# Two of four block differences moved from VectorE to GpSimd in a two-layer transformer trunk

## The reference

```
def _swiglu(h, w_gate_up, w_down):
    gu = h @ w_gate_up
    g, u = jnp.split(gu, 2, axis=-1)
    return (jax.nn.silu(g) * u) @ w_down

        h = _rmsnorm(x, norm_ffn[i])
        x = x + _swiglu(h, ffn_w_gate_up[i], ffn_w_down[i]).astype(x.dtype)
```

## Time and profile before

| | us |
|---|---|
| median of 3 runs | 2523.7 |
| lowest, highest | 2523.6, 2524.04 |
| the profiled execution's own time | 2524.11 |
| its span in the trace | 2522.0 |
| TensorE busy | 2339.1 |
| VectorE busy | 1368.0 |
| ScalarE busy | 972.9 |
| GpSimd busy | 592.3 |

### The profile page before, as it was taken

How to read it: one execution, slowest core, us unless ns; L and a number is a source line. 1 busy time by engine, 2 the same in 40 slices (tenths; PEclk the granted TensorE clock), 3 DMA queues, 4 the chain that set the end, 5 groups by cost and what they waited for, 6 DMA issues and landing times.

```text
span 2522.0 us, 33958 instructions
## 1 busy us (share of the span) xinstructions
PE 2339.1 (93%) x11188; PEld 1931.1 (77%) x11188; DVE 1368.0 (54%) x2174; ACT 972.9 (39%) x1866; POOL 592.3 (23%) x423
## 2 busy tenths in 40 slices
PE   4998999699999989999999989989699999999998
PEld 3776777588888868886888778878478888877887
DVE  7797953854444432424633489982664544543332
ACT  3116942433333421232212289982343333331223
POOL 3232424132232100020000056652223323300011
PEclk9999999799999989999999999999799999999999
DMA  5258433023222252122444687745122232252311
GB/s 188 84 173 199 96 117 117 25 76 94 80 75 88 87 216 100 59 100 68 140 137 149 179 187 168 166 124 163 38 75 75 75 100 75 75 204 83 113 50 75
DMA packets 287795, 283.38 MB, mean 112 GB/s; under 512 B 64480, under 2 KB 253280, under 8 KB 284784
## 3 DMA queue, kind: packets, MB, share of 16 engines
q1 hardware_dynamic: 267520, 225.60, 31.5%
q10 hardware_dynamic: 20208, 56.92, 6.1%
HBM read 200.63 MB, written 81.85 MB: 112 GB/s over the span
## 4 chain that ended last, share of the span: by engine, by line
PE 75%; DVE 13%; DMA 4%; ACT 3%; issue 3%; POOL 1%; ACTq 1%; SPq 0%; DVEq 0%; POOLq 0%
PE psum L1683 11%; PE psum L1684 11%; PE psum L1685 11%; PE psum L1919 11%; PE psum L1915 11%; PE psum L1917 11%; PE psum L1809 2%; DVE work_b L1574 2%; DMA set_full<-hid_scr 2%; DMA dw_raw<-in_ffn_w_down 2%; PE psum L1827 2%; PE psum L1828 1%; DVE b_lo L1398 1%; PE psum L1776 1%; PE psum L1777 1%
## 5 line engine op out<-in xcount | busy, mean ns | idle before, releaser
L1915 PE MATMUL psum<-b_hi,a_hi 128*128 128x512 f32 x1232 | 483.9, 393 | 40.0 <-DVE b_lo L1398 34.2
L1917 PE MATMUL psum<-b_lo,a_hi 128*128 128x512 f32 x1232 | 482.9, 392 | 0.0
L1919 PE MATMUL psum<-b_hi,a_lo 128*128 128x512 f32 x1232 | 482.6, 392 | 0.0
L1915 PEld LDWEIGHTS psum<-b_hi,a_hi 128*128 128x128 f32 x1232 | 233.7, 190 | 93.8 <-issue 38.9
L1683 PE MATMUL psum<-set_hi,dw_hi 128*128 128x512 f32 x704 | 278.3, 395 | 25.4 <-DVE dw_lo L1183 13.1
L1684 PE MATMUL psum<-set_lo,dw_hi 128*128 128x512 f32 x704 | 277.1, 394 | 0.0
L1685 PE MATMUL psum<-set_hi,dw_lo 128*128 128x512 f32 x704 | 276.7, 393 | 0.0
L1917 PEld LDWEIGHTS psum<-b_lo,a_hi 128*128 128x128 f32 x1232 | 233.6, 190 | 48.8
L1919 PEld LDWEIGHTS psum<-b_hi,a_lo 128*128 128x128 f32 x1232 | 233.5, 190 | 48.8
L1353 DVE TENSOR_TENSOR x_t<-psum,x_t 128x512 f32 (+1 forms) x128 | 87.6, 690 | 319.5 <-PE psum L1685 311.2
L1683 PE MATMUL psum<-h_hi,w_hi 128*128 128x512 f32 x576 | 230.8, 401 | 19.5 <-DVE w_lo L1177 14.2
(11 more groups left out here) (193 smaller groups left out, 4221.8 us busy)
## 6 DMA issues: line engine op xcount, KB each, us to landing
a_raw<-in_ffn_w_gate_up SPq DMA_DIRECT2D x88, 512.0 KB, 5.0
hid_scr<-hid_out SPq DMA_DIRECT2D x44, 512.0 KB, 5.7
dw_raw<-in_ffn_w_down SPq DMA_DIRECT2D x32, 512.0 KB, 4.1
x_scr<-x_t ACTq DMA_DIRECT2D x24, 512.0 KB, 2.7
w_raw<-in_fox_w_in SPq DMA_DIRECT2D x24, 512.0 KB, 4.0
x_t<-x_scr SPq DMA_DIRECT2D x8, 1024.0 KB, 6.0
x_t<-x_scr SPq DMA_DIRECT2D x4, 2048.0 KB, 17.8
set_full<-hid_scr SPq DMA_DIRECT2D x2, 4096.0 KB, 12.1
```

The source lines that it names most:

```text
L1915: T.matmul(out_ps, a_hi[i][:, j, :], b_hi[i][:, j, :], start=not more and j == 0, stop=False, skip_group_check=True)
L1917: T.matmul(out_ps, a_hi[i][:, j, :], b_lo[i][:, j, :], start=False, stop=False, skip_group_check=True)
L1919: last = T.matmul(out_ps, a_lo[i][:, j, :], b_hi[i][:, j, :], start=False, stop=j == KH - 1, skip_group_check=True)
```

## The change

GpSimd forms `b_full[3]`, once all four blocks are there, and `b_full[6]`, once VectorE has formed `b_full[4]`, as the first thing in its `ffn_sums`. VectorE forms `b_full[2]` and `b_full[4]` alone, so `t_dve` counts two in a layer. ScalarE waits for GpSimd ahead of `b_hi[3]` and `b_hi[6]`, and VectorE ahead of `b_lo[4]`, which overwrites what GpSimd reads for `b_full[6]`.

```
+            def block_sums(layer):
+
+                pool.wait_ge(n_done, 4 * layer + 4)
+                nc.gpsimd.tensor_tensor(b_full[3][:, :, :], n11[:, :, :], n01[:, :, :], ALU.subtract).then_inc(t_pool, 1)
+                pool.wait_ge(t_dve, 2 * layer + 2)
+                nc.gpsimd.tensor_tensor(b_full[6][:, :, :], n10[:, :, :], b_full[4][:, :, :], ALU.subtract)\
+                    .then_inc(t_pool, 1)
+
             def ffn_sums(layer):
+                block_sums(layer)
                 weight_sums(FT * layer + 1, 1)
...
                     else:
-                        act.wait_ge(t_dve, 4 * layer + (0, 0, 1, 3, 2, 3, 4)[i])
+                        act.wait_ge(t_pool if i in (3, 6) else t_dve, 2 * layer + (0, 0, 1, 1, 2, 2, 2)[i])
+                    if i == 5:
+                        act.wait_ge(n_done, 4 * layer + 4)
...
             def blocks_dve(layer, k):
-                n0, t0 = 4 * layer, 4 * layer
+                n0, t0 = 4 * layer, 2 * layer
...
                 mixed(b_full[4], n11, b_full[2])
-                mixed(b_full[3], n11, n01)
                 block_low(layer, 2, b_full[2])
                 block_low(layer, 3, b_full[3])
-                dve.wait_ge(t_dve, t0 + 2)
-                mixed(b_full[6], n10, b_full[4])
+                dve.wait_ge(t_pool, 2 * layer + 2)
                 block_low(layer, 4, b_full[4])
```

## The result

| | us |
|---|---|
| before, median of 6 runs | 2523.65 (2522.39 to 2524.36) |
| after, median of 6 runs | 2543.26 (2541.43 to 2545.66) |
| ratio | 1.0077, 95% interval 1.0064 to 1.0089 |
| profiled execution after, own time and span | 2543.78, 2541.7 |

What follows compares the result with a forecast made beforehand. The prediction took TensorE's waits on VectorE's feed-forward chain as the bound. Two layers of +4.2 us plus 1.6 us of clock made +10.0 us, forecasting 2533.7 us, range 2530 to 2538.

Steps and rivals of the forecast that it cites:

- The bound and its reach: VectorE's chain through gate_out, SiLU and the copy sets TensorE's restart at product 5; next weights shift +4.2 us per layer.
- The exclusion: In the feed-forward stretch, GpSimd's differences and VectorE instructions reading two SBUF tensors cannot run at once.
- the small case: Around 488 us before the change, VectorE lost 1.10 us to a GpSimd sum of 1.26 us (512 elements).
- The case of one PSUM operand: At 416.13 us a VectorE instruction reading PSUM and one SBUF tensor kept its 0.69 us amid GpSimd sums.
- The no-exclusion rival: Large blocks overlap on both engines; the wait before b_lo[4] decides; -3.8 us in all, 2519.9 us; chance 0.07.
- The price of a difference: One 2048-element difference on GpSimd takes 4.47 us, estimated from rows of 512 and 1024 elements.
- Hold forecast: Each moved GpSimd difference holds VectorE in the stretch for 4.3 us, 4.47 less 0.16.
- The rival with the full length: VectorE stands for GpSimd's whole 4.47 us each; +9.1, with the clock +10.7, 2534.4 us; chance 0.12.
- the dearer one: A GpSimd difference costs 5.04 us, hold 4.88; +13.9 with more clock loss, 2537.6 us; chance 0.08.
- the sentence on GpSimd's queue: Nothing but the fourth block's wait precedes the new instructions; next-round weight sums behind them shift with the rest; no cost term.
- The clock: A wait of about 3.4 us before product 5 lowers TensorE's clock in both layers, 1.6 us more in the first.
- The sum: Whole-kernel forecast: 2 x 4.2 us of VectorE shift plus 1.6 us of clock, +10.0 us; chance 0.73.

Runs made afterwards that it cites:

- the run with the sums in front: The change, with GpSimd's four second-round weight sums queued ahead of the two block differences; 2533.98 us, ratio 1.004.
- the run with the sums late: The kernel before, with GpSimd's second-round weight sums made to wait for the fourth normalised block, no difference moved; 2534.54 us, ratio 1.0043.
- the earlier copy alone: The kernel before, with ScalarE's copy of product 2 ahead of SiLU in each layer's first round, no difference moved; 2519.3 us, ratio 0.9983.

## Why the prediction was right and wrong

**The bound and its reach: right.** The chain through VectorE, `gate_out`, SiLU and the copy set TensorE's restart, and the shift of that restart went through to the end: product 5 started 8.0 us later in the first layer (8.6 of stretch less a start 0.55 earlier) and 8.6 us more in the second (1854.83 - 1836.78 = 18.05, of which 9.47 had been there at the first block, 1808.71 against 1799.24). No wait further on took any of it back: with the matmuls of both traces paired in order, those of the change start 10.87 us later at 497 us of the kernel before, and still 10.87 at 860.

**The exclusion: right.** VectorE and GpSimd exclude each other when VectorE reads two SBUF tensors and GpSimd reads any. What the small case in the trace of before showed holds for blocks four times as long: fills 0, copies 1.70 each, differences 4.35 each. The case of one PSUM operand rests on the earlier trace rows alone. The no-exclusion rival is out.

**The price of a difference: right to a few hundredths.** 4.47 was estimated from 512 and 1024 elements. In the run with the sums in front, the first difference ends at 471.52 and VectorE's instruction before it ran to 467.08 (by the start of the next), 4.44. Hold forecast 4.3, measured (19.79 - 11.09) / 2 = 4.35. (Counted from the recorded end of that VectorE instruction, 464.87 + 2.29 = 467.16, it is 4.36; the hold of 4.35 doesn't depend on this choice.) The rival with the full length is thus wrong by 0.09 at most, the dearer one (4.88) clearly. The Trainium skill ("GPSIMD Engine Reference", "Elementwise — side-by-side cycle accounting") states 4497 ns for such an instruction; the trace agrees within 0.06, or 0.14 by the other count. The Trainium skill's "SBUF — State Buffer" ("A bandwidth-pool intuition that's wrong") has the blocked side wait until 115 ns past the holder's end, measured there with VectorE as the holder. Here, with GpSimd as the holder, VectorE goes on before GpSimd's recorded end (in the same run 0.14 us before 471.52: low part 2 ends at 473.66 and takes 2.28), and the measurement decides.

**What failed: the sentence on GpSimd's queue.** The prediction said of the new instructions that the "queue holds nothing ahead of the two new instructions but the wait for the fourth block", which is true, and of what stands behind them that "GpSimd's weight sums for the next round wait for low parts of the weights, which shift with the rest". That is wrong for the second round: its sums wait for low parts of the first round's weights, which VectorE forms before the normalisation. They were free to run at 435 us and did. (The account of the kernel ahead of the prediction says what these sums wait for, but not that VectorE forms it so early.) The row at 439.42 was quoted as GpSimd's last work before the stretch; it was the fourth of exactly these sums, and the list of instructions showed them standing behind the new ones. The sum had no term for them; it is 4 x 1.08 = 4.3 us a layer, +8.6 in all, and the run with the sums late showed it alone (+4.32 a layer).

**The clock: right in kind, too small in size.** +1.6 was forecast for the first layer. After a wait of 7.05 instead of 3.4, 3.0 were lost there and 1.1 more in the second. With the sums in front (waits of 3.24 and 1.63) the first layer lost 1.6 (56 matmuls in 14.3 us) and the second none. The forecast went by the length of this one wait, and that alone doesn't decide: 2.08 us ahead of product 6 cost nothing with the earlier copy alone, 1.88 us at the same place cost 1.6 with the differences moved. What else decides stays open.

**The sum.** Forecast 8.4 + 1.6 = 10.0. In its place: 2 x (8.70 - 4.40) + 2 x 4.3 + 4.1 = 21.3, against 19.7 between the spans. The rest of -1.6 lies outside the two stretches, where the traces drift apart: at the first layer's blocks the one of after is 0.55 ahead already, and between the layers it gains another 1.5. At least 1.0 of it goes with TensorE's clock, in a stage that the change doesn't touch: there the lag of after falls from 10.5 to 9.5 us. The windows of that place, in before and 10.5 us later in after, show a granted clock of 0.83 and 0.89, and 10 matmuls more in after. Why the clock differed there stays open.

```profile
1445.00:1475.00 30.00, 22.27 (x147) 19.42 (x146) 20.73 (x58) 20.00 (x51) 15.27 (x13) 0.83 0.86 184
1455.50:1485.50 30.00, 23.03 (x157) 20.27 (x156) 21.72 (x64) 20.94 (x53) 15.76 (x14) 0.89 0.86 192
```

## What to carry to other kernels

When an instruction with a late wait is put into a queue, read what stood behind that place and when it ran before, not only what it waits for: here four small instructions, idle-time work until then, cost as much as the two that were moved. Work moved from VectorE to GpSimd leaves VectorE's path only if the two don't exclude each other there (here GpSimd's fills did not, its copies and differences did); for two-input instructions on SBUF the move costs the difference of the two prices (4.35 - 2.20 us each) instead of gaining the smaller one. And a wait on the critical chain may be one of order: letting two short instructions go first gained 8 us with no work moved.

## What the runs showed of the hardware

GpSimd's fills of 128 x 2048 float32 (1.80 us) ran beside VectorE's two-input subtractions without slowing either, while its copies (1.70 us each) and differences (4.35 us each) held VectorE. With both queues full the engines took strict turns, one instruction each: after the change each of the five low parts had one GpSimd instruction ahead of it, and neither engine got two in a row. The low parts start at 466.06, 472.57, 479.15, 482.45 and 485.75, and the total of 23.03 us is 5 x 2.20 + 0.08, two holds of 4.35 and three of 1.08, to 0.01; the fourth sum held the first low part of the next weights (1.74). A held instruction shows no idle time; only its duration tells.
